# Meta tokens without an expert, and 108 instead of 112 rows in each expert's pass

## The chip, the cores and the metric

The kernel runs on one core of one Trainium2 chip. The metric is the device time of that core in microseconds (us), the median of several executions.

## The reference

One inference step of a two-layer decoder trunk in float32. There are 336 tokens: 16 meta tokens and 256 prompt tokens in one sequence (272 positions), and 8 samples of 8 tokens. Each layer adds the output of a mixer (a state-space branch beside a sliding-window attention branch), then that of a feed-forward part. In layer 0 that part is one dense SwiGLU; in layer 1 it is a mixture of 8 experts, of which every token takes the two best:

```python
def moe_ffn(h, w_router, wg, wu, wd):
    logits = (hf @ w_router).astype(jnp.float32)
    top_v, top_i = lax.top_k(logits, TOP_K)          # TOP_K = 2 of 8
    gates = jax.nn.softmax(top_v, axis=-1)
    ...                                              # rows sorted by expert
    def one_block(args):
        xe, e = args
        return swiglu(xe, wg[e], wu[e], wd[e])       # 1024 -> 2816 -> 1024
```

The outputs are the token rows after layer 1 without those of the meta tokens (`xp[:, N_META:]`, `xs`) and the states and caches that the mixers leave. The meta tokens' rows after the last feed-forward part are read by nothing: the states and caches of layer 1 are taken before it.

## The kernel before

Tokens lie on the free axis for most of the work (1024 features are 8 chunks of 128 partitions), in three tiles where they lie on partitions: tokens 0 to 127, 128 to 255 and 256 to 335. The 16 meta tokens are the first 16 rows of tile 0. Each engine's program is written out by hand, and semaphores order them.

**Weights** stream from memory in slabs of 1 MB through a ring of 11 (`RING`), issued by SP (L434 to L440 for the fixed part, `expert_slabs` at L447 to L462 for the experts). A slab is issued when `slab_free` says that TensorE has left the one 11 before it. An expert has 33 slabs, 22 for gate and up and 11 for down.

**Routing** (VectorE, L2037 to L2101) comes after the last mixer. `route` is cleared, the token rows are copied from PSUM (L2041), the logits are scaled (L2044), the two best experts of each token are found (L2052, L2053), copied into `which` (L2056) and made into one-hot rows `oh1` and `oh2` (L2058, L2059); their sum `mm_` (L2060) goes to TensorE, whose prefix sums (L1257) number each expert's tokens and whose column sums (L1260) count them. `pick` (L2077) selects expert 0's tokens. The expert and the number in it make `row_of`, the row of each token in the memory tensor `xg_rows` (L2081 to L2089). POOL scatters the normed token rows there (L618); SP fetches the rows of the next expert during the one before (`expert_rows`, L442 to L445).

**An expert's pass** (`expert_pass` of each engine) works on `SLOTS` = 112 rows, however many tokens the expert has. TensorE does 22 x 2 x 8 x 2 matmuls of gate and up (L1305) and 22 x 8 x 2 of down (L1328). In each a weight block of 128 rows by 64 columns is loaded and the 112 columns of `xg` or `hid` move through it; the two of a pair write the lower and the upper 64 partitions of one bank. Then it turns the fetched rows of the next expert (`turn_rows`, L1278) and its own result (L1342). ScalarE takes silu of gate (L1623), VectorE multiplies by up (L2117). The result goes to `y_rows` (POOL, L623), from which two indirect loads per tile bring each token's two rows back (`rows_back`, L630). The last expert's rows go from PSUM through a selecting matmul (L1355).

If an expert has more than `SLOTS` tokens (`fullest`, from the column sums), all engines run further rounds of eight passes, up to `PASSES` = 3 in all. The memory tensors have room for them and are cleared with zeros during layer 0 (L546 to L549). Layer 1 waits for that clearing at L1679.

Of the kernel before, what the change touches and what calls it, by code (L numbers as in the profile page):

```python
# [16 lines left out]
F32 = mybir.dt.float32  # L17
U32 = mybir.dt.uint32
I32 = mybir.dt.int32
ALU = mybir.AluOpType  # L20
ACT = mybir.ActivationFunctionType
AX = mybir.AxisListType

D = 1024
DK = D // 128
LAYERS = 2
META, SEQ = 16, 256
NP = META + SEQ
SB, ST = 8, 8
NT = NP + SB * ST  # L30
# [7 lines left out]
FF = 2816  # L38
FC = FF // 128
EXPERTS = 8  # L40
SLOTS = 112
PASSES = -(-NT // SLOTS)
EPS = 1e-6
NEG = -1e30
PAST = 2048
# [12 lines left out]
UOFF = (0, NT, NT + NT - 128)  # L58
# [72 lines left out]
def bc(ap, axis, n):  # L131

    a = ap.unsqueeze(axis)
    shape = list(a.shape)
    shape[axis] = n
    return a.to_broadcast(shape)
# [52 lines left out]
def hymba_step(nc, a, o):  # L189
# [10 lines left out]
    with scope:  # L200
        def sb(name, cols, dt=F32, rows=128):
            return scope.enter_context(nc.sbuf_tensor(name, [rows, cols], dt))

        def sem(name):
            return scope.enter_context(nc.semaphore(name))
# [11 lines left out]
        row_of = sb("row_of", 6, I32)  # L217
        more_of = sb("more_of", 6, I32)
        xg_rows = nc.dram_tensor("xg_rows", [(PASSES * EXPERTS + 1) * SLOTS, D], F32, kind="Internal").ap()
        y_rows = nc.dram_tensor("y_rows", [PASSES * EXPERTS * SLOTS, D], F32, kind="Internal").ap()  # L220
        crowded = sb("crowded", 1, I32)
        router_ = sb("router", 32 * DK)
        router = router_[:, :].rearrange("p (k n) -> p k n", k=DK)
# [1 line left out]
        def C(name):  # L225
            at, n = CONST_AT[name]
            return const[:, at:at + n]

        ident, halves, turn, cosT, sinT, iota = (C(x) for x in ("ident", "halves", "turn", "cos", "sin", "iota"))
        upper, lower = C("upper"), C("lower")  # L230
# [87 lines left out]
        x_tok = arena[:, 3072:6144].rearrange("p (i n) -> p i n", i=3)  # L318
        hid = arena[:, 6144:6144 + FC * SLOTS].rearrange("p (f s) -> p f s", f=FC)
        xg_ = arena[:, 9000:9000 + DK * SLOTS]  # L320
        xg = xg_.rearrange("p (k s) -> p k s", k=DK)
        ytok = arena[0:SLOTS, 10100:11124]
        yT = arena[:, 11200:11200 + DK * SLOTS]
# [4 lines left out]
        blank = arena[0:SLOTS, 10440:10440 + D]  # L328
        ysum = arena[:, 14400:14400 + 6 * D].rearrange("p (i c n) -> p i c n", i=3, c=2)
        gsil = [arena[:, 12400 + 128 * i:12400 + 128 * i + SLOTS] for i in range(2)]  # L330
        route = arena[:, 12700:13100]
# [4 lines left out]
        def R(i, n=24, w=8):  # L336
            return route[:, i:i + n].rearrange("p (i e) -> p i e", e=w)
# [71 lines left out]
        rows_blank, rows_scattered, xrows_here = (sem(x) for x in ("rows_blank", "rows_scattered", "xrows_here"))  # L409
# [17 lines left out]
        def _(sp):  # L427
# [14 lines left out]
            def expert_rows(k):  # L442
                sp.wait_ge(rows_scattered, 16 * 3 * 2)
                sp.wait_ge(xg_psum, 2 * k + 4)
                sp.dma_start(xrows, xg_rows[SLOTS:, :].rearrange("(k s) d -> k s d", s=SLOTS)[k]).then_inc(xrows_here, 16)  # L445
# [36 lines left out]
            with sp.If(fullest > SLOTS):  # L482
                expert_rows(EXPERTS - 1)
                with sp.Fori(1, PASSES) as b:
                    with sp.Fori(0, EXPERTS) as e:
# [6 lines left out]
        def _(pool):  # L492
# [4 lines left out]
            with nc.allow_non_contiguous_dma(reason="small tables"):  # L497
# [19 lines left out]
                def load_wdt(l):  # L517
                    pool.dma_start(wdt, a["w_in"][l][:, 1536:1544].rearrange("(k p) n -> p k n", p=128)).then_inc(dtw_here, 16)

                def load_conv_rows(l):  # L520
                    pool.dma_start(conv_rows[0:24, :], a["state_conv"][l].rearrange("b r n -> (b r) n")).then_inc(conv_rows_here, 16)
# [17 lines left out]
                for l in range(LAYERS):  # L539
                    if l:  # L540
                        pool.wait_ge(hid_ready, 1)
                        load_wdt(l)
                        load_conv_rows(l)
                        pool.wait_ge(small_here, 16 * 9 * l)
                        load_tables(l)
                        pool.memset(blank[:, :], 0.0).then_inc(set_up, 1)  # L546
                        pool.wait_ge(set_up, 4)
                        pool.dma_start(xg_rows.rearrange("(s r) d -> s r d", s=SLOTS), bc(blank, 1, PASSES * EXPERTS + 1)).then_inc(rows_blank, 16)
                        pool.dma_start(y_rows.rearrange("(s r) d -> s r d", s=SLOTS), bc(blank, 1, PASSES * EXPERTS)).then_inc(rows_blank, 16)  # L549
                        for i in range(2):  # L550
                            pool.wait_ge(states_stored[i], 64 * l)
                    sample_caches(l, 0)
# [86 lines left out]
                with pool.If(fullest > SLOTS):  # L639
                    with pool.Fori(1, PASSES) as b:  # L640
                        with pool.Fori(0, EXPERTS) as e:
# [1008 lines left out]
        def _(dve):  # L1650
            v = nc.vector
            step = [0]

            def link(ins):

                step[0] += 1
                ins.then_inc(dve_step, 1)
                dve.wait_ge(dve_step, step[0])
# [16 lines left out]
            for l in range(LAYERS):  # L1675
# [8 lines left out]
                for r in range(3):  # L1684
                    ins = v.tensor_copy(raw[:, :, S0 + r:S0 + r + 78:11], bank[1][:, 0:192].rearrange("p (k b r) -> p k b r", k=DK, r=3)[:, :, :, r])
# [349 lines left out]
                dve.wait_ge(states_stored[i], 64 * LAYERS)  # L2035
            dve.wait_ge(outputs_stored, 16 * LAYERS * (2 + 2 * (3 + SB)))
            link(v.memset(route[:, 0:400], 0.0))  # L2037
            for i in range(3):
                n = TILES[i][1]
                dve.wait_ge(xtok_psum, i + 4)  # L2040
                v.tensor_copy(x_tok[0:n, i, 512:1024], bank[(4, 6, 2)[i]][0:n, :]).then_inc(xtok_ready, 1)  # L2041
# [11 lines left out]
                link(v.max_index(index8[:, 8 * i:8 * i + 8], top[:, i, :], lg[:, i, :]))  # L2053
            idx = index8[:, :].rearrange("p (i e) -> p i e", i=3)
            which = R(80, 6, 2)
            link(v.tensor_copy(which, idx[:, :, 0:2]))  # L2056
            iota8 = bc(iota[:, 0:8], 1, 3)
            v.tensor_tensor(oh1, iota8, which[:, :, 0:1].to_broadcast([128, 3, 8]), ALU.is_equal)  # L2058
            link(v.tensor_tensor(oh2, iota8, which[:, :, 1:2].to_broadcast([128, 3, 8]), ALU.is_equal))  # L2059
# [16 lines left out]
            for i, (t0, n) in enumerate(TILES):  # L2076
                ins = v.tensor_scalar(pick[0:n, i, :], iota[0:n, 0:SLOTS], gate[0:n, i, 0:1], rstd_t[0:n, i:i + 1], ALU.is_equal, ALU.mult)  # L2077
# [8 lines left out]
            v.tensor_tensor(sel[:, :, 0, :], row, oh1, ALU.mult)  # L2086
            link(v.tensor_tensor(sel[:, :, 1, :], row, oh2, ALU.mult))
            link(v.tensor_reduce(route[:, 384:390], route[:, 300:348].rearrange("p (i e) -> p i e", e=8), AX.X, ALU.add))
            v.tensor_copy(row_of[:, :], route[:, 384:390]).then_inc(placed, 1)  # L2089
            dve.wait_ge(router_here, 32)  # L2090
            dve.wait_ge(xtok_act, 3)
# [7 lines left out]
            for i, (t0, n) in enumerate(TILES):  # L2099
                ins = v.tensor_scalar(last_pick[0:n, i, :], iota[0:n, 0:SLOTS], gate[0:n, i, EXPERTS - 1:EXPERTS], g_last[2][0:n, i:i + 1], ALU.is_equal, ALU.mult)  # L2100
# [33 lines left out]
            for i, (t0, n) in enumerate(TILES):  # L2134
                for half in range(2):
                    dve.wait_ge(last_psum, 2 + 2 * i + half)
                    cols = slice(512 * half, 512 * half + 512)
                    ins = v.tensor_tensor(x_tok[0:n, i, cols], x_tok[0:n, i, cols], bank[(3, 4, 5, 6, 2, 7)[2 * i + half]][0:n, :], ALU.add)
# [60 lines left out]
```

## Time and profile before

| what | us |
|---|---|
| median of 3 executions | 1661.07 (1660.38 to 1661.41) |
| the profiled execution's own time | 1648.65 |
| its span, first to last instruction | 1647.0 |
| first matmul of expert 0 to the end of the last expert's down part, in the span | 789.5 to 1633.8 |
| TensorE matmuls busy | 1602.2 (97% of the span) |
| TensorE weight loads busy | 1348.4 (82%) |
| VectorE / ScalarE / GpSimd busy | 303.0 / 224.5 / 131.4 |
| moved by DMA | 395.23 MB, 240 GB/s over the span |

PE is TensorE's matmuls, PEld its weight loads, which overlap them. A matmul of the program leaves two matmul and two load records in the trace: the 5632 gate and up matmuls of eight experts show as 11264. A busy time is the union of records, a mean is one record from start to end, and records overlap, so the spacing of instructions is not their mean duration. The spacing is got from counts in two stretches that begin at the same moment: what is still in flight at the ends is about the same in both, and drops out of the difference.

### The profile page before, as it was taken

The numbers are of one execution on the slowest core, as the hardware profiler recorded it, in microseconds if no ns is written. First come the engines' busy times: TensorE is split into PE (matmuls) and PEld (weight loads), VectorE is DVE, ScalarE is ACT, GpSimd is POOL, SyncE is SP. The second block draws the span as 40 slices with busy tenths as digits, with TensorE's granted clock in tenths as the row PEclk, the third lists the DMA queues.
The fourth block names the chain that finished last, engine by engine and source line by source line (L and its number), as shares of the span: only waits on it lengthen the run. The fifth ranks groups of instructions, "written<-read, shape, count | busy, mean of one in ns | idle before, by whom it ended". The sixth has DMA issues, their size and how long they took to land.

```text
span 1647.0 us, 45323 instructions
## 1 busy us (share of the span) xinstructions
PE 1602.2 (97%) x20702; PEld 1348.4 (82%) x20702; DVE 303.0 (18%) x801; ACT 224.5 (14%) x655; POOL 131.4 (8%) x202
## 2 busy tenths in 40 slices
PE   7999999999999999998999999999999999999998
PEld 5667666666666667766999999999999999999997
DVE  2354630000000245453200001000000010000121
ACT  1244320000000034522100000000000000000100
POOL 3221116000000020111100000000000000000100
PEclk9999999999999899999999999999999999999999
DMA  9923238994333232223799998998989989899892
GB/s 281 238 69 93 71 115 238 361 296 154 119 111 117 75 99 74 71 94 102 253 351 334 330 382 295 346 384 289 375 309 324 394 280 373 306 353 379 303 388 71
DMA packets 192294, 395.23 MB, mean 240 GB/s; under 512 B 9698, under 2 KB 63578, under 8 KB 191952
## 3 DMA queue, kind: packets, MB, share of 16 engines
q1 hardware_dynamic: 176560, 346.31, 59.8%
q0 software_dynamic: 15168, 45.95, 9.1%
q8 instruction: 165, 2.70, 0.7%
q10 hardware_dynamic: 384, 0.13, 0.0%
q14 instruction: 17, 0.14, 0.0%
HBM read 357.23 MB, written 37.09 MB: 239 GB/s over the span
## 4 chain that ended last, share of the span: by engine, by line
PE 96%; DVE 2%; issue 1%; ACT 1%; DMA 0%; SPq 0%; DVEq 0%; ACTq 0%
PE bank L1305 33%; PE bank L1328 17%; PE bank L1217 12%; PE bank L750 6%; PE bank L1234 6%; PE bank L1053 2%; PE bank L733 2%; PE bank L1070 2%; PE bank L718 1%; PE bank L704 1%; PE bank L1026 1%; PE bank L1037 1%; PE bank L721 1%; PE bank L986 1%; PE bank L672 1%
## 5 line engine op out<-in xcount | busy, mean ns | idle before, releaser
L1305 PE MATMUL bank<-arena,ring 128*64 128x112 f32 x11264 | 547.8, 260 | 7.7 <-issue 6.7
L1305 PEld LDWEIGHTS bank<-arena,ring 128*64 128x64 f32 x11264 | 541.3, 137 | 13.8 <-issue 11.7
L1328 PE MATMUL bank<-arena,ring 128*64 128x112 f32 x5632 | 276.6, 260 | 2.1 <-issue 1.4
L1328 PEld LDWEIGHTS bank<-arena,ring 128*64 128x64 f32 x5632 | 272.0, 137 | 5.7 <-issue 4.7
L1217 PE MATMUL bank<-hnT,ring 128*128 128x336 f32 x704 | 200.6, 449 | 1.8 <-DVE hnT L1672 1.8
L1217 PEld LDWEIGHTS bank<-hnT,ring 128*128 128x128 f32 x704 | 134.8, 192 | 67.6 <-issue 3.0
L2117 DVE TENSOR_TENSOR arena<-arena,bank 128x112 f32<-128x112 f32 x176 | 47.8, 272 | 500.9 <-ACT arena L1623 500.9
L750 PE MATMUL bank<-hnT,ring 128*128 128x336 f32 x384 | 119.8, 458 | 0.0
L1623 ACT ACTIVATE arena<-bank 128x112 f32<-128x112 f32 x176 | 46.3, 263 | 509.6 <-PE bank L1305 509.6
L1234 PE MATMUL bank<-arena,ring 128*128 128x336 f32 x352 | 99.6, 446 | 0.0
L750 PEld LDWEIGHTS bank<-hnT,ring 128*128 128x128 f32 x384 | 70.8, 193 | 34.8 <-issue 6.8
L1234 PEld LDWEIGHTS bank<-arena,ring 128*128 128x128 f32 x352 | 67.0, 190 | 32.4
L623 POOL DMA_DIRECT2D y_rows<-arena x7 | 3.7, 535 | 730.9 <-DVE arena L2128 730.9
L2124 DVE COPY arena<-bank 128x448 f32<-128x448 f32 x8 | 5.0, 625 | 271.4 <-PE bank L1328 271.4
L2028 DVE TENSOR_TENSOR arena<-arena,bank 128x336 f32<-128x336 f32 x22 | 11.1, 504 | 186.9 <-PE bank L1217 186.9
L1053 PE MATMUL bank<-hnT,ring 128*128 128x336 f32 x128 | 41.1, 469 | 0.0
L1625 ACT ACTIVATE arena<-bank 128x448 f32<-128x448 f32 x8 | 4.3, 543 | 268.1 <-PE bank L1328 268.1
L1070 PE MATMUL bank<-hnT,ring 128*128 128x336 f32 x128 | 36.7, 447 | 0.0
L733 PE MATMUL bank<-hnT,ring 128*64 128x336 f32 x256 | 36.6, 447 | 0.0
L1611 ACT ACTIVATE arena<-bank 128x336 f32<-128x336 f32 x22 | 9.9, 450 | 186.1 <-PE bank L1217 186.1
L1053 PEld LDWEIGHTS bank<-hnT,ring 128*128 128x128 f32 x128 | 24.6, 198 | 12.6 <-issue 2.3
L1406 ACT ACTIVATE arena<-xT 128x336 f32<-128x336 f32 x32 | 15.4, 483 | 140.0 <-DVE xT L2031 98.9
(359 smaller groups left out, 1116.3 us busy)
## 6 DMA issues: line engine op xcount, KB each, us to landing
ring<-in_moe_w_gate SPq DMA_DIRECT2D x88, 1024.0 KB, 9.6
ring<-in_moe_w_up SPq DMA_DIRECT2D x88, 1024.0 KB, 9.4
ring<-in_moe_w_down SPq DMA_DIRECT2D x88, 1024.0 KB, 10.3
ring<-in_w_in SPq DMA_DIRECT2D x18, 1024.0 KB, 7.1
ring<-in_w_gate SPq DMA_DIRECT2D x11, 1024.0 KB, 10.8
ring<-in_w_up SPq DMA_DIRECT2D x11, 1024.0 KB, 12.7
xg_rows<-arena POOLq DMA_DIRECT2D x1, 11200.0 KB, 51.9
y_rows<-arena POOLq DMA_DIRECT2D x1, 10752.0 KB, 94.5
```

The costliest lines, as they stand in the source:

```text
L672: i = mm(bank[0][:, 0:NT], ones[:, :], squares[n][:, k, :], start=(k == 0), stop=(k == DK - 1))
L704: ins = mm(out, w[:, k, c0:c0 + 128], hnT[:, k, :], start=(k == 0), stop=(k == DK - 1))
L733: ins = mm(bank[1 + (2 + c) % 4][64 * g:64 * g + 64, 0:NT], w[:, 256 * g + 64 * c:256 * g + 64 * c + 64], hnT[:, k, :], start=(k == 0), st ...
L750: ins = mm(bank[1 + j % 2][:, 0:NT], sl(3 + j // 2)[:, k, 128 * (j % 2):128 * (j % 2) + 128], hnT[:, k, :], start=(k == 0), stop=(k == DK ...
L1053: ins = mm(bank[where][:, 0:NT], w[:, k, 128 * (i % 4):128 * (i % 4) + 128], mixT[:, 4 + k, :], start=(k == 0), stop=(k == 3))
L1070: ins = mm(bank[where][:, 0:NT], w[:, k, 128 * (i % 4):128 * (i % 4) + 128], mixT[:, k, :], start=(k == 0), stop=(k == 3))
L1217: ins = mm(bank[1 + 2 * w + f % 2][:, 0:NT], s[:, k, 128 * (f % 2):128 * (f % 2) + 128], hnT[:, k, :], start=(k == 0), stop=(k == DK - 1))
L1234: ins = mm(bank[(5, 6, 7, 1)[i]][:, 0:NT], s[:, 128 * i:128 * i + 128], hidT[:, f, :], start=(f == 0), stop=(f == FC - 1))
L1305: ins = mm(bank[3 + f % 2][rows, SLOTS * w:SLOTS * w + SLOTS], weights[:, col:col + 64], xg[:, c, :], start=(c == 0), stop=(c == DK - 1))
L1328: ins = mm(bank[5 + c // 4][rows, SLOTS * (c % 4):SLOTS * (c % 4) + SLOTS], weights[:, col:col + 64], hid[:, f, :], start=(f == 0 and c % ...
L1623: f(gsil[c % 2], bank[3 + c % 2][:, 0:SLOTS], ACT.Silu).then_inc(silu_ready, 1)
L2117: v.tensor_tensor(hid[:, c, :], gsil[c % 2], bank[3 + c % 2][:, SLOTS:2 * SLOTS], ALU.mult).then_inc(hid_ready, 1)
```

## The change

Tokens 0 to 15 are sent to no expert. For tile 0 the two expert numbers get 16 added where a constant column of `upper` is 1, which is so on the meta rows; the one-hot rows of these tokens are then all zero, and so are their counts and picks. Their entries of `row_of` point into an extra block of rows after all passes, one row for each token and choice, so that the scatter and the two indirect loads have an address; `y_rows` grows by that block. `ROUTED` is 320, and `PASSES` stays 3 (3 x 108 = 324). `SLOTS` goes from 112 to 108, and with it the moving columns of the experts' matmuls, the rows of the transfers to and from `xg_rows` and `y_rows`, and every offset that is a multiple of it.

```diff
-SLOTS = 112
-PASSES = -(-NT // SLOTS)
+SLOTS = 108
+ROUTED = NT - META
+PASSES = -(-ROUTED // SLOTS)
...
-        y_rows = nc.dram_tensor("y_rows", [PASSES * EXPERTS * SLOTS, D], F32, kind="Internal").ap()
+        y_rows = nc.dram_tensor("y_rows", [(PASSES * EXPERTS + 1) * SLOTS, D], F32, kind="Internal").ap()
...
-                        pool.dma_start(y_rows.rearrange("(s r) d -> s r d", s=SLOTS), bc(blank, 1, PASSES * EXPERTS)).then_inc(rows_blank, 16)
+                        pool.dma_start(y_rows.rearrange("(s r) d -> s r d", s=SLOTS), bc(blank, 1, PASSES * EXPERTS + 1)).then_inc(rows_blank, 16)
...
             link(v.memset(route[:, 0:400], 0.0))
+            nowhere, aside, is_meta = route[:, 392:393], route[:, 393:395], upper[:, UOFF[0] + META - 1:UOFF[0] + META]
+            v.tensor_scalar(nowhere, is_meta, float(2 * EXPERTS), None, ALU.mult)
+            link(v.tensor_tensor(route[:, 300:316], ident[:, 0:META], iota[:, 0:META], ALU.mult))
+            link(v.tensor_reduce(route[:, 395:396], route[:, 300:316], AX.X, ALU.add))
+            for c in range(2):
+                ins = v.tensor_scalar(aside[:, c:c + 1], is_meta, float(PASSES * EXPERTS * SLOTS + META * c), route[:, 395:396], ALU.mult, ALU.add)
+            link(ins)
...
-            link(v.tensor_copy(which, idx[:, :, 0:2]))
+            v.tensor_scalar(which[:, 0, :], idx[:, 0, 0:2], nowhere, None, ALU.add)
+            link(v.tensor_copy(which[:, 1:3, :], idx[:, 1:3, 0:2]))
...
             link(v.tensor_reduce(route[:, 384:390], route[:, 300:348].rearrange("p (i e) -> p i e", e=8), AX.X, ALU.add))
+            link(v.tensor_tensor(route[:, 384:386], route[:, 384:386], aside, ALU.add))
             v.tensor_copy(row_of[:, :], route[:, 384:390]).then_inc(placed, 1)
```

## Rows read from the trace of the kernel before

**Rows 1.** The page, part 1: busy time, share of the span, instructions.

```profile
PE 1602.2 (97%) x20702; PEld 1348.4 (82%) x20702; DVE 303.0 (18%) x801; ACT 224.5 (14%) x655; POOL 131.4 (8%) x202
```

**Rows 2.** The page, part 4: the chain that ended last, by line.

```profile
PE bank L1305 33%; PE bank L1328 17%; PE bank L1217 12%; PE bank L750 6%; PE bank L1234 6%; PE bank L1053 2%; PE bank L733 2%; PE bank L1070 2%; PE bank L718 1%; PE bank L704 1%; PE bank L1026 1%; PE bank L1037 1%; PE bank L721 1%; PE bank L986 1%; PE bank L672 1%
```

**Rows 3.** Groups by line and shape: busy us, mean ns, idle before.

```profile
L1305 PE MATMUL bank<-arena,ring 128*64 128x112 f32 x11264 | 547.8, 260 | 7.7 <-issue 6.7 <-ACT arena L1635 0.7
L1328 PE MATMUL bank<-arena,ring 128*64 128x112 f32 x5632 | 276.6, 260 | 2.1 <-issue 1.4
L733 PE MATMUL bank<-hnT,ring 128*64 128x336 f32 x256 | 36.6, 447 | 0.0
L721 PE MATMUL bank<-arena,hnT 128*128 128x8 f32 x64 | 7.7, 261 | 0.0
```

**Rows 4.** Stretches in expert 1: length, PE busy (instructions), clock, DMA share, GB/s.

```profile
900.00:910.00 10.00, 10.00 (x214) 1.00 0.31 98
900.00:930.00 30.00, 30.00 (x632) 1.00 0.77 269
```

**Rows 5.** Stretches of layer 0's gate and up, L1217 alone.

```profile
400.00:410.00 10.00, 10.00 (x37) 1.00 0.65 210
400.00:430.00 30.00, 30.00 (x108) 1.00 0.41 140
```

**Rows 6.** Stretches of L1043 alone, 8 columns and half loads: PE, PEld.

```profile
170.90:171.10 0.20, 0.20 (x13) 0.20 (x11) 1.00 0.50 164
170.90:171.50 0.60, 0.60 (x25) 0.60 (x25) 1.00 0.18 55
```

**Rows 7.** Who waited for whom, PEld, experts' stretch: us, times, longest.

```profile
PEld bank L1305 <- issue: 11.7, 23, 1.6
PEld bank L1328 <- issue: 4.7, 13, 0.7
```

**Rows 8.** PEld in order of time, expert 1: start, length, count, idle before.

```profile
934.10 6.14 PEld L1305 LDWEIGHTS bank<-arena,ring 128*64 128x64 f32 x128 [0.17 <-issue]
940.84 22.52 PEld L1305 LDWEIGHTS bank<-arena,ring 128*64 128x64 f32 x469 [0.60 <-issue]
```

**Rows 9.** Expert 1's gate and up, then down: all engines' busy times, clock, DMA.

```profile
895.00:963.30 68.30, 67.91 (x1407) 67.51 (x1408) 6.40 (x22) 5.82 (x22) 0.60 (x1) 1.00 0.88 314
963.30:998.60 35.30, 34.57 (x711) 33.99 (x707) 0.27 (x1) 0.81 (x2) 0.00 (x0) 1.00 1.04 391
```

**Rows 10.** SP's queue in experts' stretch: us waited, times, longest.

```profile
SPq L462 <- PE bank L1305: 414.1, 75, 29.8
```

**Rows 11.** PE in order of time, the last expert's two parts.

```profile
1527.89 31.41 PE L1305 MATMUL bank<-arena,ring 128*64 128x112 f32 x643
...
1599.49 34.28 PE L1328 MATMUL bank<-arena,ring 128*64 128x112 f32 x704
```

**Rows 12.** VectorE in order of time, routing.

```profile
769.85 1.88 DVE L2041 COPY arena<-bank 128x512 f32<-128x512 f32 x3 [1.92 <-PE bank L1087]
...
775.74 0.18 DVE L2058 TENSOR_TENSOR arena<-const,arena 128x24 f32<-128x24 f32 x1
775.84 0.18 DVE L2059 TENSOR_TENSOR arena<-const,arena 128x24 f32<-128x24 f32 x1
776.05 0.18 DVE L2060 TENSOR_TENSOR arena<-arena 128x24 f32<-128x24 f32 x1
```

**Rows 13.** The page, part 6, and the clearing's issue: us from issue to landing.

```profile
y_rows<-arena POOLq DMA_DIRECT2D x1, 10752.0 KB, 94.5
...
L549 POOL DMA_DIRECT2D y_rows<-arena x1: 1433/1433/1433, 260.8 to 260.8; - x1
```

**Rows 14.** The fetch of an expert's rows: issue (SP), its median landing, its reader.

```profile
920.89 0.34 SPq L445 DMA_DIRECT2D arena<-xg_rows  x1
...
arena<-xg_rows SPq DMA_DIRECT2D x7, 448.0 KB, 12.2
...
998.60 0.99 PE L1278 MATMUL bank<-const,arena 112*128 112x112 f32 x8
```

## The prediction

> **What bounds the kernel now.** I read the page's busy shares first: TensorE's matmuls fill 97% of the span, no other engine over 18% [rows 1]. The chain that ended last confirms it: half of it is the experts' two matmul lines, L1305 and L1328 [rows 2]. So the question is what paces one of these matmuls, and there are three candidates: its columns, its weight load, and the weights' arrival.
>
> The spacing comes from counts. Between 910 and 930 us expert 1 started 632 - 214 = 418 records in 20 us, 47.85 ns each [rows 4]. The two halves of a pair run side by side: L733, also in halves, needs 36.6 us / 256 = 143 ns a record at 336 columns, so 286 a pair, and the full-width matmul of 336 columns needs 20 us / (108 - 37) = 281.7 [rows 3, 5]. So I count in pairs: 95.7 ns at 112 columns, 281.7 at 336. The slope is 186.0 / 224 = 0.830 ns a column, which is two cycles at the granted 2.4 GHz (clock 1.00 in these stretches), and 95.7 - 112 x 0.830 = 2.7 ns is fixed.
>
> The load could hide behind that line, so I looked for matmuls with hardly any columns. L1043 has the same half loads and 8 columns: 12 matmul records in 0.4 us, or 67 ns a pair (the load records, 14 in 0.4 us, give 57). L721, 8 columns with full loads, needs 7.7 us / 64 = 120 ns a record [rows 3, 6]. The floor of the half loads, 67 at most, is under 92; that of full loads would not be. So at 112 columns the experts are paced by columns and still would be at 108.
>
> The Trainium skill, TensorE: Matmul & The Clock Gate, section LDWEIGHTS, puts a load at its columns / 1.2 in ns: 53 for 64 columns, 107 for 128. By that rule, the trace agrees: both lie below the spacings just read, by 4 to 14 ns, and the half loads stay hidden.
>
> The weights' arrival: gate and up of expert 1 draw 314 GB/s at a DMA share of 0.88, down 391 at 1.04 [rows 9]. In down the DMA engines are full. Yet SP waits 414.1 us for TensorE to leave slabs, behind L1305 alone [rows 10], so the ring is ahead. An expert takes (1527.89 - 895.0) / 6 = 105.5 us from start to start [rows 9, 11], and moves (68.3 x 314 + 35.3 x 391) / 103.6 = 340 GB/s on average; at the 391 that the engines do reach the same bytes would need 105.5 x 340 / 391 = 91.7 us. A pass will still take about 102. The transfers bind only locally.
>
> **The change part by part.** The sum is against the profiled execution, 1648.65 us; it is 12.4 us under the median of the runs, 1661.07, and no row says where those lie. I carry the difference over unchanged.
>
> 1. *Four columns fewer.* (11264 + 5632) / 2 = 8448 pairs [rows 3] x 4 x 0.830 ns = **-28.0 us**. All of it is on the path: PE is busy 67.91 of 68.30 us in a part [rows 9].
> 2. *turn_rows* moves 108 columns of the identity: 7 x 8 = 56 records x 3.3 ns = **-0.2 us**. The result's turning (L1342) loads fewer columns and moves 128 as before: 0. L1267 has full loads, whose 120 ns with 8 columns lie above 112 x 0.830 + 2.7: 0.
> 3. *Stalls of "issue".* Weight loads stood idle 36 times for 16.4 us with nothing in the profile to wait for [rows 7]. They sit where the DMA engines are full, and a run of 128 records, 6.14 us, lies between two of them [rows 8], as if something were fetched for each such run and came late. That run will take 64 x 3.3 = 0.21 us less. If what comes late keeps its own time, each stall grows by up to 0.21: 36 x 0.21 = 7.6 us. If its request moves with TensorE, 0. More stalls may join as the engines fill further: I bound that by as much again, 15 us in all; below, I allow 2 us of shrinking. I take the middle of the first two, **+3.8 us**.
> 4. *The last expert.* The rows come back to `ysum` in its gate and up part, which takes 1599.49 - 1527.89 = 71.6 us against 68.3 in expert 1 [rows 9, 11]: here transfers do press. Its saving is 704 pairs x 3.32 ns = 2.3 us. Between losing nothing and all of it I take **+0.5**, since the ring starts this part full.
> 5. *Routing.* The five added instructions after the clearing of `route` and the three waits of their chain cost some 0.2 us for each wait and 0.1 for the others (L2058 to L2060 start 0.10 and 0.21 apart), 0.8 in all. VectorE idles 1.92 us there for TensorE (769.85) [rows 12]: 0, and at most 0.8 if that cover went. The split copy into `which` adds one start, **+0.1**, on TensorE's path to the prefix sums. The addition before `row_of` (0.2) delays the scatter; the fetch is issued at 920.9, some 130 us later, and `pick` is made before it: 0.
> 6. *Transfers.* The fetch for the next expert lands after 12.2 us and is read 998.60 - 920.89 = 77.7 us after issue [rows 14]; even six times that would be hidden. The clearing of `y_rows` (2700 rows after, 2688 before) lands at 260.8 + 94.5 = 355.3 [rows 13]; its waiter is in layer 1, and layer 0's gate and up still run at 430 us [rows 5], with the down part to follow: at least 75 us of cover. Bytes of the weights are the same. 0, and I see no gain.
> 7. *ScalarE and VectorE* work 4 columns less per block; they idle between blocks: 0.
>
> The Trainium skill, DMA: Bandwidth & Descriptors, section "Why a DMA increments its semaphore by 16 and not by 1", speaks against the change: a transfer is spread over the largest number of engines up to 16 that divides its slowest dimension. 112 rows would use 16 engines with 7 rows each, 108 only 12 with 9. No row here shows 108 rows; by the rule the clearing would land at 260.8 + 94.5 x 16 / 12 = 387 (an estimate), still 43 us ahead of that 430, so it leaves the sum as it is.
>
> Sum: -28.0 - 0.2 + 3.8 + 0.5 + 0.1 = **-23.8 us**: 1624.8 for the profiled execution, **1637.3 us** as a median (ratio 0.986).
>
> **The rivals.**
>
> *R1, the gain is given back to the DMA engines.* They are already full in every down part and at the last expert. With a faster TensorE more stalls appear and the slabs' lead shrinks until some are waited for. For it: share 1.04, and the 36 stalls. Against: the average need stays 10 us an expert (102 against 91.7) below what the engines reach, and SP waits on TensorE. Give-back of 8 to 20 us: 1641 to 1653, middle 1647.
>
> *R2, 108 columns are paid like 112.* Rows show 8, 112 and 336 columns, all multiples of 8, and none shows that the 0.830 holds between steps of 8 or 16. Then only terms 2 to 5 are left, within 1 us: about 1661.
>
> *R3, most of the spacing isn't columns.* The same page on TensorE, section Back-to-back issue gap, has a sustained roofline of 81 ns at 128 and 131 at 512 columns, where load and matmul set the spacing together. As a mechanism here it would be a load that overlaps only in part, so that the spacing runs from the 67 ns at 8 columns to 95.7 at 112: 28.7 / 104 = 0.276 ns a column, 9.3 us saved, 1651.8. Against: 112 and 336 then wouldn't lie on a line with 2.7 ns fixed. By the page's own slope, 50 / 384 = 0.13 ns, it would be 4.4 us (an estimate).
>
> *R4, slower: rows of 432 bytes stream worse than rows of 448.* `xg`, `hid` and the two halves of a bank start at multiples of SLOTS x 4 bytes: 448 = 7 x 64, 432 isn't a multiple of 32. If each matmul paid for its columns as for 128, a pair would take 128 x 0.830 + 2.7 = 108.9 ns, +13.2 x 8448 = +112 us: 1773. It decides from 3.3 ns a pair on, where it eats term 1. Nothing in the trace speaks for it, and nothing excludes it, as no matmul row has such an offset.
>
> *R5, the change doesn't do what it says:* an expert with over 108 tokens would start eight more passes for each further round, some 840 us each. The reference's router on its own inputs gives counts of 75, 66, 86, 75, 98, 75, 77, 88 without the meta tokens (104 at most with them), so ten more tokens fit. Under 1 in 100.
>
> **How the numbers follow.** Forecast, saving 20 to 28 us (1633 to 1641): 0.78. Saving more, up to 31, with fewer stalls: 0.03. R1: 0.10. R2: 0.04. R3: 0.02. R4 with R5: 0.03. The range from 1631.5 to 1647 holds the forecast, most of the better case and half of R1, 0.85; its ends are terms 1 to 5 with stalls shrinking by 2 us or less, and the 15 us of term 3. About 0.2%, 3.3 us, is what a measurement can tell from no change. Faster by more: 0.78 + 0.03 + 0.10 + 0.02 = 0.93; same: R2, 0.04; slower: 0.03.
>
> **What would show it.** Right: in a stretch like 910 to 930 the counts give 46.2 ns a record (433 in 20 us), and the two groups' busy times fall from 547.8 and 276.6 to about 530 and 267; the idle time of issue is 16 to 24 us; VectorE still waits before its copies at L2041. R1: the same spacing but more idle time before L1305 and L1328, and DMA shares near 1 in gate and up. R2: 47.8 ns a record. R3: 47.3. R4: above 47.8, at L1305 and L1328 alike. R5: more than 11264 records. The prediction is wrong in size if the stalls of term 3 change by more than 8 us, or if the 12.4 us outside the profiled execution change.

## The result, and the profile after

The changed kernel takes 1649.73 us as a median of 20 executions (1643.01 to 1655.81), the kernel before, now also over 20, 1658.66 (1653.67 to 1662.63). The ratio is 0.9947, 95% interval 0.9933 to 0.9960: 8.9 us faster, 6.6 to 11.1 by the interval. The forecast was 23.8 us and 1637.3, so the sign was right and the size was not; the time lies above the range.

The two profiled executions even go the other way: a span of 1652.3 us after against 1647.0 before. That is the first thing to read, because the sum was made on that one page.

The page of the kernel after: its span, busy times, and its two costly lines (L1306 and L1329 answer to L1305 and L1328) with idle time before them and what ended most of it.

```profile
span 1652.3 us, 45330 instructions
PE 1591.9 (96%) x20702; PEld 1330.8 (81%) x20702; DVE 303.2 (18%) x808; ACT 223.7 (14%) x655; POOL 132.5 (8%) x202
...
L1306 PE MATMUL bank<-arena,ring 128*64 128x108 f32 x11264 | 537.4, 258 | 16.1 <-issue 14.9
L1306 PEld LDWEIGHTS bank<-arena,ring 128*64 128x64 f32 x11264 | 528.1, 138 | 25.3 <-issue 22.8
L1329 PE MATMUL bank<-arena,ring 128*64 128x108 f32 x5632 | 269.9, 256 | 8.0 <-issue 7.1
L1329 PEld LDWEIGHTS bank<-arena,ring 128*64 128x64 f32 x5632 | 262.9, 137 | 14.2 <-issue 13.9
```

There are as many records as before, so no further round of passes ran. Two stretches of expert 1 that begin together give the spacing, as [rows 4] did (length, PE busy and records, clock, DMA share, GB/s):

```profile
910.00:920.00 10.00, 10.00 (x221) 1.00 0.28 79
910.00:940.00 30.00, 30.00 (x654) 1.00 0.76 270
```

654 - 221 = 433 records in 20 us, 46.2 ns each, against 47.85 before. That is the number that the prediction gave for two cycles a column. So the four columns were saved in full where TensorE isn't stopped; over all records that spacing is worth 28 us. What came in their place is idle time of "issue" before the weight loads, in the experts' stretch of the kernel after (us, times, longest), which answers to [rows 7]:

```profile
PEld bank L1306 <- issue: 22.8, 35, 1.5
PEld bank L1329 <- issue: 13.9, 30, 1.2
```

36.7 us in 65 stalls, where the page of before had 16.4 in 36. In the down parts the number went from 13 to 30. A run of loads between two stalls has the shape that the prediction described (start, length, records, idle before):

```profile
1572.48 5.93 PEld L1306 LDWEIGHTS bank<-arena,ring 128*64 128x64 f32 x127 [0.42 <-issue]
1579.39 5.93 PEld L1306 LDWEIGHTS bank<-arena,ring 128*64 128x64 f32 x128 [0.98 <-issue]
1585.74 5.93 PEld L1306 LDWEIGHTS bank<-arena,ring 128*64 128x64 f32 x127 [0.42 <-issue]
1592.64 5.93 PEld L1306 LDWEIGHTS bank<-arena,ring 128*64 128x64 f32 x128 [0.97 <-issue]
```

128 records in 5.93 us instead of 6.14 [rows 8], and a stall ahead of each. From 1572.48 to 1592.64, three such pieces took 20.16 us, 6.7 each, though TensorE worked through one in 5.9.

The weights are not what it waits for. SP still stands behind TensorE, for 423.0 us ([rows 10] had 414.1):

```profile
SPq L463 <- PE bank L1306: 423.0, 79, 35.7
```

A smaller part lies around the start of expert 0. This is the stretch there in which the granted clock was at half (1.2 GHz), after and then before (length, PE busy and records, clock, DMA share, GB/s):

```profile
779.40:803.30 23.90, 19.93 (x132) 0.50 0.32 119
```

```profile
775.00:785.10 10.10, 7.11 (x35) 0.50 0.01 2
```

In the changed kernel's profiled execution TensorE ran at half its clock for 23.9 us here, in the other for 10.1. From the 3500th to the 3700th matmul record, a span that holds most of this stretch, it took 44.7 us after and 40.1 before. These are single executions. Of the other kernels with 108 rows below, light108 and spaced108 have the 23.9 us too, and cols108_rows112, slots108_only and paced_spaced108 have about 10; their medians don't differ accordingly, so it isn't shown to be a cost of the change.

### The profile page after: what moved, and what is told of

Its sections match the earlier page's. It is cut to its first block, busy times and chain, and to the rows that moved or that the text cites. A ratio compares the mean times of both kernels' runs of the same rounds, so it can differ in the third digit from the quotient of the medians.

```text
span 1652.3 us, 45330 instructions
## 1 busy us (share of the span) xinstructions
PE 1591.9 (96%) x20702; PEld 1330.8 (81%) x20702; DVE 303.2 (18%) x808; ACT 223.7 (14%) x655; POOL 132.5 (8%) x202
## 4 chain that ended last, share of the span: by engine, by line
PE 95%; issue 2%; DVE 2%; ACT 1%; DMA 0%; SPq 0%; DVEq 0%; ACTq 0%
PE bank L1306 32%; PE bank L1329 16%; PE bank L1218 12%; PE bank L751 6%; PE bank L1235 6%; PE bank L1054 3%; PE bank L734 2%; PE bank L1071 2%; PE bank L719 1%; PE bank L705 1%; PE bank L1027 1%; PE bank L1038 1%; PE bank L722 1%; PE bank L1268 1%; PE bank L987 1%
## 5 line engine op out<-in xcount | busy, mean ns | idle before, releaser
L1306 PE MATMUL bank<-arena,ring 128*64 128x108 f32 x11264 | 537.4, 258 | 16.1 <-issue 14.9
L1306 PEld LDWEIGHTS bank<-arena,ring 128*64 128x64 f32 x11264 | 528.1, 138 | 25.3 <-issue 22.8
L1329 PE MATMUL bank<-arena,ring 128*64 128x108 f32 x5632 | 269.9, 256 | 8.0 <-issue 7.1
L1329 PEld LDWEIGHTS bank<-arena,ring 128*64 128x64 f32 x5632 | 262.9, 137 | 14.2 <-issue 13.9
L2127 DVE TENSOR_TENSOR arena<-arena,bank 128x108 f32<-128x108 f32 x176 | 47.0, 267 | 502.7 <-ACT arena L1624 502.7
L1624 ACT ACTIVATE arena<-bank 128x108 f32<-128x108 f32 x176 | 45.8, 260 | 508.2 <-PE bank L1306 499.4
L2134 DVE COPY arena<-bank 128x432 f32<-128x432 f32 x8 | 4.9, 607 | 271.1 <-PE bank L1329 271.1
L2029 DVE TENSOR_TENSOR arena<-arena,bank 128x336 f32<-128x336 f32 x22 | 11.1, 504 | 187.0 <-PE bank L1218 187.0
L1626 ACT ACTIVATE arena<-bank 128x432 f32<-128x432 f32 x8 | 4.2, 530 | 267.3 <-PE bank L1329 267.3
L1071 PE MATMUL bank<-hnT,ring 128*128 128x336 f32 x128 | 36.7, 446 | 0.0
## 6 DMA issues: line engine op xcount, KB each, us to landing
ring<-in_moe_w_gate SPq DMA_DIRECT2D x88, 1024.0 KB, 10.1
ring<-in_w_gate SPq DMA_DIRECT2D x11, 1024.0 KB, 10.6
ring<-in_w_up SPq DMA_DIRECT2D x11, 1024.0 KB, 12.5
y_rows<-arena POOLq DMA_DIRECT2D x1, 10800.0 KB, 113.5
```

What stands on the lines that cost most here:

```text
L1071: ins = mm(bank[where][:, 0:NT], w[:, k, 128 * (i % 4):128 * (i % 4) + 128], mixT[:, k, :], start=(k == 0), stop=(k == 3))
L1306: ins = mm(bank[3 + f % 2][rows, SLOTS * w:SLOTS * w + SLOTS], weights[:, col:col + 64], xg[:, c, :], start=(c == 0), stop=(c == DK - 1))
L1329: ins = mm(bank[5 + c // 4][rows, SLOTS * (c % 4):SLOTS * (c % 4) + SLOTS], weights[:, col:col + 64], hid[:, f, :], start=(f == 0 and c % ...
L1624: f(gsil[c % 2], bank[3 + c % 2][:, 0:SLOTS], ACT.Silu).then_inc(silu_ready, 1)
L2127: v.tensor_tensor(hid[:, c, :], gsil[c % 2], bank[3 + c % 2][:, SLOTS:2 * SLOTS], ALU.mult).then_inc(hid_ready, 1)
```

## The experiments

The theories. **T1**: the program of a faster TensorE reaches it late, more often and by more. T1a puts that down to full DMA engines, T1b to the speed alone. **T2**: transfers of 108 rows, on fewer DMA engines, are to blame. **T3**: the routing part costs it. **T4**, formed after the first four runs: indirect transfers issued back to back starve TensorE's fetch. **T5**: the pieces that arrive late are 16 KB of program.

All ratios are to the kernel before on the same chip. Its medians there were 1658.86 us beside again, cols108_rows112, meta_only and slots108_only, 1658.71 beside light112, light108, cols100_rows112 and spaced108, and 1660.06 beside the rest. "Issue idle" is that of the weight loads before the two expert lines in the profiled execution.

| kernel | columns | median us | ratio, 95% | issue idle, gate and up + down, us (times) |
|---|---|---|---|---|
| before | 112 | 1658.66 | 1 | 11.7 + 4.7 (36) |
| again | 112 | 1657.35 | 0.9989 (0.9971 to 1.0007) | 18.5 + 3.4 (41) |
| meta_only | 112 | 1656.53 | 0.9982 (0.9968 to 0.9997) | 18.4 + 4.5 (41) |
| after | 108 | 1649.73 | 0.9947 (0.9933 to 0.9960) | 22.8 + 13.9 (65) |
| cols108_rows112 | 108 | 1651.94 | 0.9961 (0.9943 to 0.9978) | 27.3 + 12.9 (68) |
| slots108_only | 108 | 1649.28 | 0.9944 (0.9926 to 0.9962) | 23.6 + 13.3 (70) |
| cols100_rows112 | 100 | 1640.10 | 0.9893 (0.9864 to 0.9921) | 50.3 + 30.3 (95) |
| light112 | 112 | 1650.93 | 0.9957 (0.9937 to 0.9976) | 15.2 + 0 (20) |
| light108 | 108 | 1631.11 | 0.9828 (0.9800 to 0.9857) | 18.8 + 0.7 (28) |
| spaced112 | 112 | 1645.42 | 0.9916 (0.9897 to 0.9935) | 11.8 + 4.0 (29) |
| spaced108 | 108 | 1637.20 | 0.9875 (0.9838 to 0.9912) | 14.2 + 13.4 (50) |
| paced_spaced108 | 108 | 1636.89 | 0.9875 (0.9854 to 0.9897) | 16.9 + 7.2 (36) |
| spaced100 | 100 | 1631.55 | 0.9819 (0.9796 to 0.9843) | 40.7 + 28.9 (83) |
| fat112 | 112 | 1729.71 | 1.0421 (1.0397 to 1.0445) | 72.7 + 13.6 (78) |

**again.** The kernel before, without an edit.

> The kernel before once more, for what two executions of the same program differ by. All theories: ratio 1.000 within 0.002. T1 (TensorE's program reaches it late when the DMA engines are full) says that the idle time of issue before the loads of the experts' two matmul lines is again 12 to 20 us and the spacing 47.85 ns a record. If it were instead over 30 us, the one profile of before was a lucky one, and part of the loss seen after the change isn't the change's.

The ratio is that of no change. But its profiled execution has a span of 1661.3 us, 14 more than the first, and 21.9 us of issue idle, just over the 12 to 20 that T1 said. The first one, 1648.65 us, lies below every one of the 20 executions whose median is 1658.66: the page that I summed on was of an unusually quick one. Part of its luck shows in expert 7, in the loads of the kernel run again, and POOL beside them:

```profile
1549.38 0.29 PEld L1305 LDWEIGHTS bank<-arena,ring 128*64 128x64 f32 x5 [0.20 <-issue]
1550.13 0.19 PEld L1305 LDWEIGHTS bank<-arena,ring 128*64 128x64 f32 x3 [0.46 <-issue]
1550.86 0.29 PEld L1305 LDWEIGHTS bank<-arena,ring 128*64 128x64 f32 x5 [0.54 <-issue]
1552.30 0.22 PEld L1305 LDWEIGHTS bank<-arena,ring 128*64 128x64 f32 x4 [1.15 <-issue]
1553.73 0.31 PEld L1305 LDWEIGHTS bank<-arena,ring 128*64 128x64 f32 x4 [1.21 <-issue]
...
1547.91 0.97 POOL L630 DMA_INDIRECT arena<-y_rows,row_of  x1 [0.30 <-issue]
1549.18 0.94 POOL L630 DMA_INDIRECT arena<-y_rows,row_of  x1 [0.30 <-issue]
1550.43 0.94 POOL L630 DMA_INDIRECT arena<-y_rows,row_of  x1 [0.30 <-issue]
```

While POOL issues its indirect transfers, TensorE gets a handful of instructions, stops for about a microsecond, gets another handful. Then its clock falls to half. By the mean of 0.81 in the first of these two stretches that was at about 1552.7, and it lasts to 1559.5:

```profile
1549.00:1555.00 6.00, 3.44 (x30) 0.81 0.91 315
1555.00:1559.50 4.50, 4.35 (x47) 0.50 0.99 239
```

The profile of after has the same at 1541 to 1550; that of before hasn't it, and its stalls came to 16.4 us only [rows 7]. Counted from the same matmul record to the same, the execution of again loses 3.0 us before the experts, 6.3 around the scatter in expert 0, and 5.6 in expert 7; between these two experts the distance changes by under 1 us.

**cols108_rows112.** The change, but with transfers and tensors of 112 rows an expert, and 4 zero rows in `ytok`.

```diff
+ROWS = 112
...
-        ytok = arena[0:SLOTS, 10100:11124]
+        ytok = arena[0:ROWS, 10100:11124]
...
-                sp.dma_start(xrows, xg_rows[SLOTS:, :].rearrange("(k s) d -> k s d", s=SLOTS)[k]).then_inc(xrows_here, 16)
+                sp.dma_start(xrows, xg_rows[ROWS:, :].rearrange("(k s) d -> k s d", s=ROWS)[k]).then_inc(xrows_here, 16)
```

> The whole change, but every transfer to and from xg_rows and y_rows keeps 112 rows, so only the matmuls, copies and picks have 108 columns. T2 (transfers of 108 rows use fewer of the DMA engines, and those delay what TensorE fetches) expects the lost gain back: 22 to 28 us faster than before, ratio 0.983 to 0.987. T1 (the loss comes with the faster TensorE itself) expects what the change gave, 6 to 12 us faster, ratio 0.993 to 0.996, with issue stalls of some 35 us.

T2 falls: 0.9961 is no better than the change's 0.9947. The clearing of the tensors did slow down with 108 rows. Part 6 of the page of after has

```profile
xg_rows<-arena POOLq DMA_DIRECT2D x1, 10800.0 KB, 76.3
y_rows<-arena POOLq DMA_DIRECT2D x1, 10800.0 KB, 113.5
```

where `y_rows` took 94.5 before [rows 13] and `xg_rows` 51.9; with 112 rows again, in cols108_rows112, they are 93.6 and 51.3. The Trainium skill's rule on the engines of a transfer (DMA: Bandwidth & Descriptors, "Why a DMA increments its semaphore by 16 and not by 1") gave 126 as an estimate; the measured 113.5 goes its way, less far. As predicted nobody waited for it.

**meta_only.** `SLOTS = 112` in the changed kernel.

> The routing part of the change alone: meta tokens go to no expert, but a pass has 112 rows. T1 and T2: no difference, ratio 0.999 to 1.001. T3 (the routing instructions or the rows set aside cost the missing time, by a later start of expert 0 or by the scatter) expects 8 to 20 us slower, 1.005 to 1.012.

0.9982: no loss from the routing, T3 falls. It lies a little under the 0.999 to 1.001 of T1 and T2, and the upper end of the interval is 0.9997; a gain of 2 us has no reason that I can name and is below what I would call shown.

**slots108_only.** `SLOTS = 108` in the kernel before, nothing else.

> 108 rows alone, with the meta tokens still routed (the fullest expert has 104 tokens, so nothing is left out); PASSES becomes 4, which makes the two cleared tensors a third larger. T1 and T2: like the change, 6 to 12 us faster, ratio 0.993 to 0.996. T3: 22 to 28 us faster, 0.983 to 0.987.

0.9944, the change's 0.9947. The whole effect is that of the 108 rows.

**light112 and light108.** Of each down slab of the experts half the columns are loaded; the matmuls read what is in the slot.

```diff
-                        src = a["moe_w_down"][0, e, r0:r0 + 256, :].rearrange("(r p) n -> p r n", p=128)
+                        src = a["moe_w_down"][0, e, r0:r0 + 256, 0:512].rearrange("(r p) n -> p r n", p=128)
+                        dst = dst[:, :, 0:512]
```

> The kernel before, but of every down slab of the experts only the left half of the columns is loaded, so an expert brings 28.8 MB in place of 34.6; the matmuls are the same and the result isn't the reference's. T1a (TensorE's program comes late because the DMA engines are full): the stalls of experts 1 to 6 in their down parts, 6.5 us in this kernel with all weights, go to under 1, and the time falls by 8 to 15 us, ratio 0.991 to 0.995. T1b (it comes late because TensorE runs through a chunk of it faster than it can be brought, however idle the engines are): no change, ratio 0.999 to 1.001.

> The changed kernel with the same half of every down slab left out. T1a: the difference to light112 is the whole 28 us that the columns give, or at least 24, so 36 to 43 us under before, ratio 0.974 to 0.979. T1b: the difference to light112 stays 9 to 12 us.

At 112 columns the lighter load gives 7.8 us, at 108 it gives 1649.73 - 1631.11 = 18.6, so 112 to 108 is worth 19.8 us here and 8.9 with all weights. T1b alone can't be: it allowed no change at 112. T1a gets the direction, and the stalls of the down parts go to 0 as it said, but not the size: it said 8 to 15 us at 112, and at least 24 for the step to 108.

The parts show where. This is the time from the first to the last matmul record of a part, summed over the eight experts, in the profiled executions ("half" is half of each down slab loaded):

| down slabs | columns | gate and up, us | down, us |
|---|---|---|---|
| whole | 112 (mean of before, again, meta_only) | 560.1 | 276.1 |
| whole | 108 (mean of after, cols108_rows112, slots108_only) | 554.1 | 275.3 |
| whole | 100 (cols100_rows112) | 541.4 | 273.3 |
| half | 112 (light112) | 558.5 | 270.4 |
| half | 108 (light108) | 546.8 | 261.5 |

Four columns are worth 18.7 us in gate and up and 9.3 in down by term 1. With whole slabs the down parts gain 0.8 of the 9.3, and with 12 columns fewer 2.8 of 28; with half slabs they gain 8.9. One of these parts closely, expert 1's in the kernel after (end of gate and up at 974.0), and then in light108:

```profile
974.00:1009.70 35.70, 33.84 (x706) 32.75 (x702) 0.27 (x1) 0.79 (x2) 0.00 (x0) 1.00 1.04 392
```

```profile
966.90:999.60 32.70, 32.70 (x710) 32.68 (x706) 0.27 (x1) 0.77 (x2) 0.00 (x0) 1.00 0.98 340
```

With the DMA engines at 0.98 and 340 GB/s TensorE is busy every moment, and the part takes 32.7 us. At 1.04 and 392 GB/s it takes 35.7, and the 3 us are stalls. Before, the same part was 35.3 [rows 9]. A share of 1.04 doesn't always cost that much: expert 2's down part in the kernel after lasts 33.3 us.

```profile
1077.70:1111.00 33.30, 32.94 (x710) 32.68 (x706) 0.27 (x1) 0.72 (x2) 0.00 (x0) 1.00 1.04 393
```

What T1a missed lies in gate and up, whose weights all come in both kernels: these parts gain 11.7 us of the 18.7, and light108 keeps 18.8 us of stalls in them. How much of that is due to full engines the two runs don't tell.

**cols100_rows112.** The same as cols108_rows112 with `SLOTS = 100`.

> The whole change with 100 columns in place of 108 (the fullest expert has 98 tokens), transfers of 112 rows. The columns alone would give 84 us. T1a: the stalls grow with each step, since the 391 GB/s that the DMA engines reach want 91.7 us for an expert and this TensorE would want 92.5: 20 to 50 us faster than before, ratio 0.970 to 0.988, idle time of issue over 60 us and slabs waited for. T1b: each run of 128 records loses the same 0.2 us again for 4 columns, so a third of the gain is kept: 25 to 35 us.

12 columns would be 84 us; the stalls took about 60 of it (80.6 us, against 20.4 as the mean of the three profiles at 112 with unspaced transfers), and 18.6 remain. That lies under T1a's range of 20 to 50, which the interval only reaches into (0.9864 to 0.9921 against 0.988), and outside T1b's, which it doesn't reach. What T1a said of waits for slabs didn't come: nearly all of the loads' idle time is still that of issue.

**spaced108 and spaced112.** Each indirect transfer of the scatter and of the first `rows_back` waits for the one before to land.

```diff
                                                 in_=hn_tok[0:n, i, :], in_offset=None).then_inc(rows_scattered, 16)
+                        pool.wait_ge(rows_scattered, 16 * (2 * i + c + 1))
...
                                                     in_offset=bass.IndirectOffsetOnAxis(ap=rows[0:n, 2 * i + c:2 * i + c + 1], axis=0)).then_inc(y_here[i], 16)
+                            if one_by_one:
+                                pool.wait_ge(y_here[i], 16 * (c + 1))
```

> The changed kernel, with each of the six indirect transfers of the scatter and of the first rows_back issued only when the one before has landed. In three of the four profiles so far TensorE stands still for 5 to 7 us in pieces of 0.5 to 1.3 us while they are issued back to back, in expert 0 and in expert 7, and its clock then falls to 1.2 GHz. T4 (these issues starve what TensorE fetches): 6 to 14 us faster than the changed kernel, ratio to before 0.986 to 0.991. Against T4: no difference to the changed kernel, 0.993 to 0.996.

> The kernel before with the indirect transfers issued one by one. T4 (the back-to-back issues starve TensorE's fetch in experts 0 and 7) expects a gain of 5 to 12 us here too, ratio 0.993 to 0.997, and then the difference between spaced112 and spaced108 is what the 108 columns bring without that effect: 28 us less the growth of the stalls in experts 1 to 6, 28 - 9 = 19 us or less. If spaced112 doesn't differ from before, the starving belongs to the 108 columns alone, and the difference is 22 us or more.

The forecast of T4 holds: 12.5 us against the changed kernel, and 14.6 against before at 112 columns, somewhat more than the 5 to 12 expected there. POOL now issues one each 8 us (spaced108):

```profile
1544.51 0.94 POOL L632 DMA_INDIRECT arena<-y_rows,row_of  x1 [8.21 <-DMA arena<-y_rows,row_of]
1552.58 0.94 POOL L632 DMA_INDIRECT arena<-y_rows,row_of  x1 [7.13 <-DMA arena<-y_rows,row_of]
```

and the issue idle of gate and up fell from 22.8 us to 14.2. So this cost is one of both kernels, and not what ate the gain: 1645.42 - 1637.20 = 8.2 us is all that 108 columns bring here too, or 21.5 - 14.6 = 6.9 if each is taken against the kernel before on its own chip.

**spaced100.** Both edits.

> cols100_rows112 with the indirect transfers issued one by one. T4: 8 to 14 us under cols100_rows112, so 27 to 33 us under before, ratio 0.980 to 0.984.

28.5 us under before and 8.6 under cols100_rows112, as expected. It has the lowest ratio of all runs, 0.9819.

**paced_spaced108.** SP's loop over the experts unrolled, and a wait for the slab three before.

```diff
+                    if j >= 3 and isinstance(k, int):
+                        p = j - 3
+                        sp.wait_ge(slab_here[(MOE0 + p) % RING], k * (16 * FFN_SLABS // RING) + (fixed_seen[(MOE0 + p) % RING] + 16 * (p // RING + 1)))
```

> spaced108, and SP sends an expert's slab only when the one three before it has landed, so that at most three are on their way; SP's loop over the experts is unrolled for it. T1a (the stalls come from full DMA engines): what is on its way at a time falls, but the engines stay as busy, since three are enough to fill them; if the length of the queue before them delays the fetch, the stalls fall by half and the time by 5 to 10 us against spaced108. If only being busy matters, within 3 us of spaced108.

0.9875, the same as spaced108, so neither the 5 to 10 us came nor can the times of the two kernels be told apart. In its profiled execution the down parts' stalls are 7.2 us instead of 13.4 and those of gate and up 16.9 instead of 14.2; its eight down parts take 268.7 us instead of 275.6. But that execution took 1626.55 us, the quickest of five, and isn't one to build on. Whether a shorter queue of slabs helps stays open; the medians show no effect.

**fat112.** The kernel before, with two waits more in TensorE's program for each pair of matmuls in gate and up.

```diff
+                            pe.wait_ge(set_up, 3)
+                            pe.wait_ge(ident_here, 16)
                             for half in range(2):
                                 rows, col = slice(64 * half, 64 * half + 64), 128 * in_group + 64 * half
```

> The kernel before, and in TensorE's gate and up part two more waits for each pair of matmuls, on semaphores that have long reached their value: 12.5 or 25% more program there, nothing else. T5 (TensorE's program is fetched in pieces of 16 KB, and what stalls it is that a piece doesn't come while it works through the one before) expects more stalls in gate and up at the same 47.85 ns a record, and 20 to 60 us more in all, ratio 1.012 to 1.036, with the instruction queue's packets up from 165 by 10 to 25. If the program's size has nothing to do with it, the ratio is 0.999 to 1.002.

69.7 us slower than before on its chip, more than the 20 to 60 of T5. T5's marks are there. The instruction queue, before (its first page) and here:

```profile
q8 instruction: 165, 2.70, 0.7%
```

```profile
q8 instruction: 176, 2.88, 0.7%
```

2.70 MB in 165 packets are 16 KB each, and there are 11 more. The trace has 48139 - 45323 = 2816 instructions more, one for each of the 8 x 352 pairs of matmuls in gate and up: of the two waits only one made an instruction of its own. 11 x 16384 / 2816 = 64 bytes is what an instruction takes. The loads between two stalls:

```profile
946.03 5.56 PEld L1307 LDWEIGHTS bank<-arena,ring 128*64 128x64 f32 x114 [0.88 <-issue]
953.03 5.46 PEld L1307 LDWEIGHTS bank<-arena,ring 128*64 128x64 f32 x113 [1.44 <-issue]
```

114 and 113 records instead of 128: 128 / 1.125 = 113.8, one instruction more for each eight. Where it isn't stalled, TensorE keeps nearly its pace (208 records in 10 us, 48.1 ns):

```profile
1140.00:1150.00 10.00, 10.00 (x210) 1.00 0.45 162
1140.00:1160.00 20.00, 20.00 (x418) 1.00 0.63 222
```

So a run of 128 loads, with its 128 matmuls, 256 instructions of 64 bytes, is one 16 KB piece of TensorE's own program, and the stall behind it is the next piece coming late. The Trainium skill states the size in Runtime: NRT & Kernel Launch, Terms: an engine's instruction memory is refilled in 16 KiB blocks. By that rule, the trace agrees, at 16 KB a packet and with the 113.8. The stalls of the down parts rose too, to 13.6 us, though nothing was added there; that is not explained.

The packets themselves can be seen in the kernel before. During gate and up of expert 1 (895.0 to 963.3), with its 1408 loads [rows 9], the instruction queue brought 11, and 1408 / 128 is 11:

```profile
q8 instruction: 11, 0.18, 1.0%
```

The packed trace has the start and the length of every packet. All 36 stalls of [rows 7] end 1.2 to 1.6 us after one of these packets has landed, where one moment in twelve would do so by chance. After the change 59 of the 65 do. The packet's own transfer takes 1.1 us, late or not, so what is late is its start.

The 6 others of after (3.6 us) are short stops between 1541 and 1547, beside the indirect transfers issued back to back. TensorE starts only 1 to 5 loads between two of them, not 128, and a single packet comes in the whole stretch. So there are two kinds of stop. The late pieces cost 16.4, 14.7 and 15.6 us in before, again and meta_only, and 33.1, 32.8 and 28.8 in after, cols108_rows112 and slots108_only. The stops at the indirect transfers cost 0, 7.2 and 7.3 there, and 3.6, 7.4 and 8.1 here; in the three kernels spaced112, spaced108 and paced_spaced108 none is left. They go away when the transfers are spaced, as T4 said, but that they come from the fetch of the program, T4's reason, is not shown, and the counts speak against it.

## Why the prediction was wrong

**What bounds the kernel.** Right for a pass without stalls: columns, two cycles each, not the half loads. The spacing of 46.2 ns was forecast and measured, and with it R2 (47.8), R3 (47.3) and R4 (above 47.8) fall; R5 falls with the count of records. But the list of three candidates lacked the fourth, the arrival of TensorE's own program, though term 3 had seen its trace.

**Term 1** (-28.0) right by the spacing. The busy times went to 537.4 and 269.9, not to 530 and 267. The profile of after has stretches at half the clock in experts 0 and 7; in that of paced_spaced108, with 108 columns and none in the experts, they are 528.2 and 266.9.

**Term 3** is the step that failed. It took +3.8 between 0 and 7.6, with 15 as the outer bound. Measured: the mean of the three profiles at 112 columns with unspaced transfers is 20.4 us, that of the three at 108 is 37.9, so **+17.5**, of which 16.0 are late pieces of program and 1.5 stops at the indirect transfers. -28.0 + 17.5 - 0.2 + 0.1 is -10.6, against the 8.9 measured (6.6 to 11.1). The outer bound was summed wrong besides: with 15 us in place of 3.8 the sum gives 1648.5, not the 1647 at which the range ends, and the measured 1649.7 is above both. Two faults are in the term. I multiplied the 0.21 us by the 36 stalls that there were, as if the other pieces had time to spare; the right bound is all (11264 + 5632) / 128 = 132 pieces, 28 us, the whole gain. In the down parts 30 of 44 pieces stall now, where 13 did, and these parts kept 275.3 of their 276.1 us. And "its request moves with TensorE, so 0" had no row behind it. "The next piece comes no earlier, however fast TensorE is" would have been the plain reading for the down parts, where the engines are full, and it is what they show. The sentence that the stalls sit where the engines are full was itself only half right: 23 of the 36, 11.7 of 16.4 us, lay in gate and up [rows 7], where expert 1 has a share of 0.88.

**Terms 2, 5, 6, 7** right as far as seen: meta_only shows no loss from routing, VectorE still waits before its copies (1.07 us, from 1.92), cols108_rows112 shows no loss from the rows' transfers.

**Term 4** can't be told from the changed kernel: what the indirect transfers cost in expert 7 is larger than both its ends. With them spaced, expert 7's gate and up part takes 70.1 us at 112 columns and 69.2 at 108, a saving of 0.9 where the term left 1.8, in one execution each.

**R1** was the case that came true: the same spacing, more idle time of issue, a give-back of 8 to 20 us. It had 0.10, mainly on the argument that the average need stays 10 us an expert under what the engines reach. That argument is right for the slabs, which nobody waits for, and says nothing of a 16 KB piece that must come within 6 us. Its mechanism was partly off as well: the slabs' lead never ran out, and expert 1's gate and up part has a DMA share of 0.89, hardly more than the 0.88 before, where R1 expected shares near 1.

**The 12.4 us** between profile and median, carried over as a constant, were a warning (10.0 by the median of 20). Of the 14.3 us between the two profiled executions of this kernel 11.9 lie at the indirect transfers of experts 0 and 7 and in the half clock after them, which the first execution was spared. So the sum stood on a page with 16.4 us of stalls where the two others at 112 columns have 21.9 and 22.9.

Left open: why a packet of program starts late while the DMA engines are busy, what stops TensorE while indirect transfers are issued back to back (the runs show that spacing them helps, not through which resource), how much of the stalls in gate and up is due to full engines, and what the executions without a profile look like inside.

## What to carry to other kernels

When one engine is near 100% busy with thousands of small instructions, its program is a stream like the weights: divide the program's bytes by the time and look for idle time of "issue" at equal counts of instructions. If such stalls are there, shortening each instruction is worth little while the DMA engines are full (0.8 of 9.3 us in the down parts here); fewer bytes moved beside them gave that gain back (8.9), and more instructions cost much, so fewer should be worth trying, which no run here did. An edit that multiplies a per-instruction saving by thousands needs its give-back bounded by all the pieces of program, not by those that stall today. And a profile whose own time lies below those of all other executions is to be taken again before summing on it.

## What was not expected of the hardware

- One more instruction for each eight in TensorE's gate and up part, each doing nothing, cost 69.7 us: 86.3 us of issue idle against 16.4 to 22.9, at a spacing of 48.1 against 47.85 ns.
- Six indirect transfers issued back to back by GpSimd stop TensorE for 0.2 to 1.3 us at a time over some 5 us, and its clock then falls to 1.2 GHz. Issuing each when the last has landed brings 14.6 us at 112 columns and 12.5 at 108.
- The eight down parts with whole slabs (DMA share 1.04 in experts 1 and 2) take 276.1 us at 112 columns, 275.3 at 108 and 273.3 at 100. With half slabs (0.98 in expert 1, 327 and 340 GB/s) they take 270.4 and 261.5, and TensorE hardly stops.
- Every late piece of program lets TensorE go on 1.2 to 1.6 us after it has landed; its own transfer takes 1.1 us.
